# Two decoder layers, fp32 split products, one core: the rotary product leaves TensorE and the transfers exchange the halves

## The reference, cut to what matters

```python
def partial_rope(x, pos):
    half = ROPE_DIM // 2                     # 8
    ...
    x1, x2, rest = xf[..., :half], xf[..., half:ROPE_DIM], xf[..., ROPE_DIM:]
    out = jnp.concatenate([x1 * cos - x2 * sin, x2 * cos + x1 * sin, rest], axis=-1)
```

## Time and profile before

| | us |
|---|---|
| median of 3 runs | 1254.49 (1252.92 to 1254.75) |
| the profiled execution's own time | 1252.77 |
| its span, first to last instruction | 1251.0 |
| TensorE busy | 1235.3 |
| VectorE busy | 1028.7 |
| ScalarE busy | 699.1 |
| GpSimd busy | 172.2 |

### The profile page before, as it was taken

The page is one execution under the profiler, slowest core; times in us unless marked ns, Lnnn a source line. Parts: engine busy times, 40 slices in busy tenths (PEclk is TensorE's granted clock), DMA queues, the critical chain, the costliest instruction groups (busy, mean ns, idle before and its releaser), DMA issues.

```text
span 1251.0 us, 23751 instructions
## 1 busy us (share of the span) xinstructions
PE 1235.3 (99%) x9344; PEld 1182.2 (95%) x9344; DVE 1028.7 (82%) x1692; ACT 699.1 (56%) x1158; POOL 172.2 (14%) x120
## 2 busy tenths in 40 slices
PE   7999999999999999999999999999999999999999
PEld 7899999999999999999998989888899999998998
DVE  5787789578999999897655898885889999989865
ACT  6566547655555555763354774485655555558332
POOL 2464213100000000000015462131000000000000
DMA  5322210132332221223323222110322332222333
GB/s 196 98 74 69 68 35 21 49 118 85 115 122 102 102 102 69 69 102 118 110 94 100 92 68 69 34 52 18 134 102 102 118 119 102 102 69 85 118 118 118
DMA packets 27451, 113.74 MB, mean 91 GB/s; under 512 B 3664, under 2 KB 4304, under 8 KB 21968
## 3 DMA queue, kind: packets, MB, share of 16 engines
q1 hardware_dynamic: 26624, 111.18, 26.0%
q10 hardware_dynamic: 720, 1.09, 0.2%
HBM read 108.79 MB, written 2.10 MB: 89 GB/s over the span
## 4 chain that ended last, share of the span: by engine, by line
PE 90%; DVE 2%; POOL 2%; issue 1%; ACT 1%; DMA 0%; SPq 0%; POOLq 0%; DVEq 0%; ACTq 0%
PE ps L1390 22%; PE ps L1396 11%; PE ps L1005 10%; PE ps L1107 5%; PE ps L1101 5%; PE ps L1011 5%; PE ps L1102 5%; PE ps L1474 5%; PE ps L1510 4%; PE ps L1231 3%; PE ps L1479 2%; PE ps L1515 2%; PE ps L1204 1%; PE ps L1179 1%; PE ps L1214 1%
## 5 line engine op out<-in xcount | busy, mean ns | idle before, releaser
L1101 PE MATMUL ps<-xhi,whi 128*128 128x264 f32 (+1 forms) x616 | 174.3, 311 | 0.0
L1102 PE MATMUL ps<-xlo,whi 128*128 128x264 f32 (+1 forms) x616 | 167.5, 300 | 0.0
L885 POOL TENSOR_TENSOR wlo<-raw,whi 128x1024 fp32r<-128x1024 f32 x48 | 118.8, 2478 | 179.3 <-ACT whi L1688 178.7
L1101 PEld LDWEIGHTS ps<-xhi,whi 128*128 128x128 f32 x616 | 116.1, 188 | 4.8 <-issue 0.8
L1102 PEld LDWEIGHTS ps<-xlo,whi 128*128 128x128 f32 x616 | 116.2, 189 | 3.5
L1688 ACT ACTIVATE whi<-raw 128x1024 fp32r<-128x1024 f32 x74 | 77.9, 1054 | 48.3 <-PE ps L1011 29.9
L1107 PE MATMUL ps<-xhi,wlo 128*128 128x264 f32 (+1 forms) x616 | 100.6, 305 | 0.4 <-POOL wlo L885 0.4
L1107 PEld LDWEIGHTS ps<-xhi,wlo 128*128 128x128 f32 x616 | 85.3, 188 | 4.9 <-POOL wlo L885 0.6
L1390 PE MATMUL ps<-fhi,hi_a 128*128 128x264 f32 (+1 forms) x352 | 88.2, 283 | 0.0
L1390 PE MATMUL ps<-flo,hi_a 128*128 128x264 f32 (+1 forms) x352 | 88.1, 282 | 0.0
L1390 PE MATMUL ps<-flo,hi_b 128*128 128x264 f32 (+1 forms) x320 | 80.3, 283 | 0.0
(11 more groups left out here) (373 smaller groups left out, 3856.7 us busy)
## 6 DMA issues: line engine op xcount, KB each, us to landing
raw<-in_weights SPq DMA_DIRECT2D x116, 512.0 KB, 3.5
raw<-in_groups SPq DMA_DIRECT2D x42, 1024.0 KB, 4.8
out_hT<-h SPq DMA_DIRECT2D x7, 256.0 KB, 4.6
h<-in_hT SPq DMA_DIRECT2D x4, 264.0 KB, 6.2
h<-in_hT ACTq DMA_DIRECT2D x4, 264.0 KB, 5.9
cst<-in_consts SPq DMA_DIRECT2D x1, 780.5 KB, 9.3
xnb<-feat SPq DMA_DIRECT2D x20, 33.2 KB, 2.0
feat<-xnb SPq DMA_DIRECT2D x20, 33.2 KB, 2.0
```

Source lines behind the costliest of these rows:

```text
L885: nc.gpsimd.tensor_tensor(wlo[:, b], raw[:, b], whi[:, b].bitcast(F32), ALU.subtract).then_inc(split_done, 1)
L1101: nc.tensor.matmul(o, whi[:, k % 2, n], xhi[:, n, cut], start=(n == 0), stop=False)
L1102: nc.tensor.matmul(o, whi[:, k % 2, n], xlo[:, n, cut], start=False, stop=False)
```

## The change

The host lays the 16 rotated features of a head at every fourth row (0, 4, 8, ... of the 64), the two partners of a pair next to each other, and the gains of the norms likewise. `gather` copies a tile's 32 rotated rows in one transfer into buffer 0, and the same rows with partners exchanged in two transfers of 16 rows into buffer 1. TensorE's rotation step and its constant matrix are gone; VectorE multiplies buffer 0 by cosine, then waits for the exchanged rows and multiplies buffer 1 by a table of sines that carries the sign, and adds. `spread` puts 32 rows back in one transfer. The letters F leave TensorE's strings and the two digits of the rotation leave `BANKS_OF` in each layer; all other letters and digits are the same. The table of constants is 128 columns narrower.

```diff
-C_ID, C_ONE, C_BLK, C_ROT, C_COS, C_SIN = 0, 128, 256, 384, 512, 512 + N
+C_ID, C_ONE, C_BLK, C_COS, C_SIN = 0, 128, 256, 384, 384 + N
...
-ROPE_ROWS = (slice(48, 64), slice(112, 128))
+ROPE_ROWS = slice(0, 128, 4)
+ROPE_PAIR = (slice(0, 128, 8), slice(4, 128, 8))
...
-    "gather": (DMAE,), "rope": (PE, DVEE), "spread": (DMAE,), "split_k": (ACTE, DVEE),
+    "gather": (DMAE,), "rope": (DVEE,), "spread": (DMAE,), "split_k": (ACTE, DVEE),
...
-        self.packed = [sem(f"packed{n}_of{l}") for n in range(2)]
+        self.packed = sem(f"packed_of{l}")
+        self.exchanged = sem(f"exchanged_of{l}")
...
-                        sp.wait_ge(ev.spread[0], 16 * 6)
+                        sp.wait_ge(ev.spread[0], 16 * len(ROPED[0]))
+                    sp.dma_start(xnb[at:at + 32, 0], feat[ROPE_ROWS, place(k)]).then_inc(ev.packed, 16)
                     for hh in range(2):
-                        row = at + 16 * hh
-                        sp.dma_start(xnb[row:row + 16, 0], feat[ROPE_ROWS[hh], place(k)]).then_inc(ev.packed[n], 16)
+                        sp.dma_start(xnb[at + hh:at + 32:2, 1], feat[ROPE_PAIR[1 - hh], place(k)]).then_inc(ev.exchanged, 16)
 
                 def spread(n):
 
                     sp.wait_ge(ev.roped, n + 1)
                     for k in ROPED[n]:
-                        for hh in range(2):
-                            row = group_rows(k)[1] + 16 * hh
-                            sp.dma_start(feat[ROPE_ROWS[hh], place(k)], xnb[row:row + 16, 0]).then_inc(ev.spread[n], 16)
+                        row = group_rows(k)[1]
+                        sp.dma_start(feat[ROPE_ROWS, place(k)], xnb[row:row + 32, 0]).then_inc(ev.spread[n], 16)
...
-                def rope(n):
-                    b0, done = job_begin(("rope", n))
-                    pe.wait_ge(ev.packed[n], 32 * len(ROPED[n]))
-                    m = 32 * len(ROPED[n])
-                    for hf in range(2):
-                        ins = nc.tensor.matmul(bank(b0 + hf, HALF, slice(0, m)), cols(C_ROT, m, slice(0, m)),
-                                               xnb[0:m, 0, hf * HALF:(hf + 1) * HALF], start=True, stop=True)
                     ins.then_inc(done, 1)
 
...
-                    act.wait_ge(ev.spread[0], 16 * 6)
+                    act.wait_ge(ev.spread[0], 16 * len(ROPED[0]))
...
                 def rope(n):
-                    b0, taken, m = wait_done(("rope", n))
+                    tiles = sum(len(roped) for roped in ROPED[:n + 1])
                     dve.wait_ge(cst_loaded, 16 * (l + 1))
+                    dve.wait_ge(ev.packed, 16 * tiles)
                     rows = slice(0, 32 * len(ROPED[n]))
                     x, other = xnb[rows, 0], xnb[rows, 1]
-                    nc.vector.tensor_tensor(halves(other), two_banks(b0)[rows], halves(cols(C_SIN, N, rows)), ALU.mult).then_inc(taken, 1)
                     chain(nc.vector.tensor_tensor(x, x, cols(C_COS, N, rows), ALU.mult))
-                    dve.wait_ge(taken, m)
+                    dve.wait_ge(ev.exchanged, 32 * tiles)
+                    chain(nc.vector.tensor_tensor(other, other, cols(C_SIN, N, rows), ALU.mult))
                     nc.vector.tensor_tensor(x, x, other, ALU.add).then_inc(ev.roped, 1)
...
-def turned_last(w):
-
-    return np.roll(w.reshape(w.shape[0], -1, 64), -16, axis=2).reshape(w.shape)
+def turned_apart(w):
+
+    heads = w.reshape(w.shape[0], -1, 64)
+    out = np.empty_like(heads).reshape(w.shape[0], -1, 16, 4)
+    out[..., 0] = heads[..., :16].reshape(-1, heads.shape[1], 2, 8).swapaxes(2, 3).reshape(-1, heads.shape[1], 16)
+    out[..., 1:] = heads[..., 16:].reshape(w.shape[0], -1, 16, 3)
+    return out.reshape(w.shape)
...
-            p[l, :, c] = np.tile(np.roll(g[l], -16 if c in (P_DQ, P_DK) else 0), 2)
+            p[l, :, c] = np.tile(turned_apart(g[l][None])[0] if c in (P_DQ, P_DK) else g[l], 2)
...
-        c[r, C_COS:C_COS + N] = np.cos(ang[r % half])
-        c[r, C_SIN:C_SIN + N] = np.sin(ang[r % half])
-        c[r ^ half, C_ROT + r] = 1 if r // half % 2 else -1
+        c[r, C_COS:C_COS + N] = np.cos(ang[r // 2 % half])
+        c[r, C_SIN:C_SIN + N] = np.sin(ang[r // 2 % half]) if r % 2 else -np.sin(ang[r // 2 % half])
...
```

More of the change, by code:

```diff
@@ L223 @@
 PROJ_AT = [{s: n for n, s in enumerate(proj_halves(l))} for l in range(DEPTH)]
-AUX_KINDS = ("prenorm", "norm", "rope", "turn_tile", "gate", "index", "logits", "turn", "meta_turn", "turn_k", "gla_att", "gla_out",
+AUX_KINDS = ("prenorm", "norm", "turn_tile", "gate", "index", "logits", "turn", "meta_turn", "turn_k", "gla_att", "gla_out",
              "gla_kv", "back")
-WIDE_KINDS = ("prenorm", "norm", "rope", "turn_tile", "gate", "turn_k", "gla_att", "gla_out")
+WIDE_KINDS = ("prenorm", "norm", "turn_tile", "gate", "turn_k", "gla_att", "gla_out")
 def width_of(job):
@@ L257 @@
 STEPS_OF = (
[L258 to L261, removed]
+    {PE: "AAAAAAAAAAAABAAADAAAAAAAAAAAALAAAAAAAAADAMAAMDAAMMMMMMAAMAMAADAAAAAAADAPAAAAAAAAPAAXAXAAXADXAAALAaAL"
+     "AAbAdDAAAAAXAXAXXAXXAaAXAAYXYbMAXMAAAAAadMAMAZYZXYAXZYXZAYXbAAAAdZYXZAZYAAXLAPAZRAARPALYXAYAXMaAMabA"
+     "AAdLZZYAXYXZZbYAXYdZAAYAZZXXYXAYALXATSRSaAAATRTRSSATTaZbYXAdZADAZYAXYXDZYXAZbAYdDZAAAAYaZDYZAXXZAAXb"
+     "AYdAXAYXaZYXZYXZYXZbYadZYZYZfZbfdfff",
      ACTE: "ABCADAPALHIHACIADCIMIMDMMMMMMCAMMDAJCODIPIAJAPCXIIXDCXXALaPLADeJJXAXXXXAaXYYMMAXXXaMMYXeYYYAXPXeAYXK"
@@ L281 @@
 BANKS_OF = (
[L282 to L285, removed]
+    "0220230230123232020230130302030130130102310230020121021201320202020123020320301320130213031010130020"
+    "201202301201230320121203020230203013020301232",
+    "0222012032030032020123012301020201032013201302301320302020202020131020130113013031203103120103123012"
+    "320320120202301130130101302032013",
 )
@@ L1337, in out @@
                             low_pass(n, n, 2 * n + hf, parts[hf], mix_tiles, ks, True).then_inc(half_done, 2 // len(parts))
-                do = dict(prenorm=prenorm, proj=proj, norm=norm, rope=rope, turn_tile=turn_tile, turn_k=turn_k, gate=gate,
+                do = dict(prenorm=prenorm, proj=proj, norm=norm, turn_tile=turn_tile, turn_k=turn_k, gate=gate,
                           index=index, logits=logits, turn=turn, values=values, meta_turn=meta_turn,
@@ L1778, in split_q_hi @@
                     k, hh = SPLIT_Q[n]
-                    act.wait_ge(ev.spread[n // 4], 16 * (4 if n >= 4 else 6))
+                    act.wait_ge(ev.spread[n // 4], 16 * len(ROPED[n // 4]))
                     if n in SPLIT_AFTER:
@@ L1865, in fox_log @@
                     chain(nc.scalar.activation(fox_gate(), fox_gate(), ACT.Identity, bias=par[fox_rows, P_FB:P_FB + 1]))
-                    act.wait_ge(ev.spread[1], 16 * 4)
+                    act.wait_ge(ev.spread[1], 16 * len(ROPED[1]))
                     f = xnb[fox_rows, 0]
```

15 lines of the change are left out of this document (7 added, 8 removed).

## The result

The changed kernel takes 1256.54 us (median of 10 runs, 1255.64 to 1258.09) against 1254.28 us for the kernel before (10 runs beside it, 1252.91 to 1255.01): a ratio of 1.0019, 95% interval 1.0011 to 1.0027. It is slower by 2.3 us where 3.0 us less were forecast, and it lies above the range. The profiled execution took 1255.89 us, its span is 1254.0 us; the one before had 1252.77 and 1251.0 us.

What follows compares the result with a forecast made beforehand. The prediction took TensorE, busy 99% of the span, to bound the kernel. Gains of 0.5 + 1.2 (layer 0) and 0.2 + 1.1 (layer 1) make 3.0 us: 1254.49 to 1251.5 us, range 1248.4 to 1254.3 us.

Steps and rivals of the forecast that it cites:

- What the change offers: TensorE time around the four rotation products: 1.85 and 1.71 us in layer 0, 1.27 and 1.24 in layer 1, 6.07 in all.
- SyncE's queue: Gather and spread transfers: strided rows issue in 0.62 us and land in 2.0 us; the later unit load costs nothing.
- Layer 0, 1.7 us forecast: Both rotations of layer 0: 1.7 us gained, between 0.5 and 3.56 us.
- the chain from the projection halves: Layer 0, ScalarE to VectorE up to the first index scores: only 0.5 us of 1.85 us is left.
- the forecast wait of 0.5 us: Layer 0, norm of unit 6: TensorE, 2.2 us ahead, meets GpSimd's squares with 1.7 us of slack; waits about 0.5 us.
- so 0.2 us of 1.27 us is left: Layer 1, first rotation: GpSimd's subtraction holds one VectorE operation, the turn of SMALL waits about 1 us; gain 0.2 us.
- The lock: Layer 1, first rotation: VectorE operations with two SBUF inputs contend with GpSimd's subtraction; without it, 1.1 us better.
- Layer 1, second rotation, 1.1 of 1.24 us forecast: VectorE's unbroken run moves only 0.2 us, returning rows come over 1 us earlier; gain 1.1 us, not under 0.2.
- D: Rival: SyncE takes longer to issue strided rows, up to 1.10 us each; 4.7 us slower, 1259.2 us; chance 0.08.
- C: Rival: the lock does not bite in layer 1; gain 4.1 us, 1250.4 us; chance 0.15.
- A: Rival: all offered time arrives, 6.07 us, giving 1248.4 us; chance 0.13.
- B: Rival: mostly given back, in layer 0 the sum meets GpSimd's squares; gain 1.4 us, 1253.1 us; chance 0.27.

Runs made afterwards that it cites:

- e1: Kernel before with the new row layout and one packing and one return transfer per tile, product kept in both layers: 1250.20 us, ratio 0.9968.
- e12: Same kernel as e1, run again beside e9 to e11: 1250.62 us, ratio 0.9971.
- e8: Changed kernel with the change in layer 0 alone; layer 1 keeps its product, with the new layout: 1252.34 us, ratio 0.9986.
- e10: e8 with GpSimd's subtraction for unit 7 in layer 0 held until VectorE has split the keys: 1250.19 us, ratio 0.9968.
- e3: Changed kernel with GpSimd's subtraction for unit 5 in layer 1 put after the first rotation's sum: 1252.65 us, ratio 0.9992.
- e2: Changed kernel with VectorE's two copies of unit 3 put ahead of layer 1's first rotation: 1254.49 us, ratio 1.0004.
- e5: Kernel before with VectorE's sine product of layer 1's first rotation done seven times instead of once: 1260.36 us, ratio 1.0052.
- e4: Changed kernel with GpSimd's subtractions for units 4 and 5 in layer 1 put after the first rotation: 1254.09 us, ratio 1.0003.
- e9: Layer 0 as in e1 (new layout, product kept), layer 1 as in e7 (no product): 1249.83 us, ratio 0.9964.
- e11: e7 with GpSimd's subtraction for unit 7 in layer 0 held until VectorE has split the keys: 1250.25 us, ratio 0.9967.
- e7: e4 with SyncE's spread of the first group in layer 1 put ahead of the unit load: 1251.96 us, ratio 0.9983.

## Why the prediction was wrong

**What the change offers.** The product is gone, with its 16 records; and TensorE's rows bear out the time offered: it gets ahead by 1.8 us at each product of layer 0 and by 1.28 us at the first of layer 1 (1.85, 1.71 and 1.27 us offered).

**SyncE's queue** was costed rightly for layer 0: issue 0.59 us, landing 2.0 us, and the load behind the gathers, issued 2 us later, delays nothing that a trace shows. At the first gathers of layer 1 the landing is longer, 2.7 us in the median and up to 4.5 us (before 2.7 and 3.6). That the cosine product still began at 664.08 us, inside the forecast 663.9 to 664.4, is luck: the last tile's packed rows were issued at 660.70 us and not near 661.8, since layer 0 had ended earlier, and took 3.4 us instead of 2.0. What the step missed is the worth of packing with one transfer, a part of this change: 1.5 us in layer 0. With the order of VectorE and GpSimd that came with it, e1 and e12 are 3.8 and 3.6 us under before with the product in place. Of the 1.85 us offered at the first product, 0.73 were a wait for transfers that half as many issues remove.

**Layer 0, 1.7 us forecast.** Measured 1.75 in the table, 1.6 by e8; the sum knows no lower clock, which takes 1.0 us off it in some executions. The size was right and its reasons only half. I put the loss at the first index scores down to the chain from the projection halves, where only 0.5 us could be had. TensorE did wait there, 1.1 us; but e10 shows that 2 us of the chain are a subtraction in its way, in the kernel before too, where the split that I took for the chain's own length stood at 2.91 us for work of 0.70. I had read the 0.23 us of waiting behind it and not the row itself. At the norm of unit 6 the forecast wait of 0.5 us came, as 0.8 us, but for ScalarE's relu of an index score and not for GpSimd's squares.

**Layer 1, first rotation, "so 0.2 us of 1.27 us is left": this step failed.** The lock was foreseen, with its place and size (cosine product forecast until 667.1, it ended at 665.76, 1.35 us earlier with the whole layer; turn's wait about 1.1 us; e3, which has that one hold alone, waits 1.4 us). But I let one subtraction meet the rotation, the one that stood there before, and kept the next at its old 668.75. It waits for ScalarE's rounding, that waits for TensorE's buffer, and TensorE was what the change made earlier, against the layer's own beginning by 1.28 us, the very time I was counting as gain. So it came at 666.12 and held the sum as well, and the turn waited 3.3 us. To this came 1.6 us of lower clock, of which the prediction has nothing. In the profiled executions of e2, after, and e5 the clock fell here behind waits of 2.15, 3.3 and 3.8 us, and in those of e3 and e4 with 1.42 and 1.80 us it didn't. The length of a wait does not settle it, though: in layer 0 it fell behind 1.1 us in three executions out of seven. e3 takes out the second hold and with it both costs: 3.9 us by the medians, 3.6 us with each against the kernel before beside it, of the 5.0 us between the forecast and the result.

The Trainium skill (page "SBUF — State Buffer", section "Who interferes with whom") had the rule, that two SBUF inputs on VectorE contend with a GpSimd instruction that reads SBUF; the traces agree, 1.68 and 2.75 us instead of 0.71. It was applied to the instructions as they stood and not as the change would move them.

**Layer 1, second rotation, 1.1 of 1.24 us forecast.** It gave nothing. VectorE's run is unbroken there, and it came late from the first rotation, by 2.2 us (its second rotation starts at 697.45 instead of 695.23); TensorE waits 0.9 us for it. Even in e9 and e11, where the first rotation is in order, that wait of 0.9 us stands. So the term was too large by most of itself, and not only by what came from in front. The rows point to the same step as in the first rotation: the prediction let VectorE's run move as one piece, and it grew. In after, e3, e7, e9 and e11 GpSimd's subtraction and squares hold two of its operations (2.05 and 1.13 us, shown above) that take 0.48 and 0.23 us where layer 1 keeps its product, and the stretch takes 9.95 to 9.97 us. With the new layout and the product (e1, e8, e10, e12) it is 9.2 to 9.4 us, and TensorE, later by the product, does not wait. That the growth is what makes the wait is read from the traces; no run moved that subtraction or those squares.

**The rivals.** D is out by the issues' durations; C by the lock's biting; A by e11, where with no subtraction in the way of layer 1's first rotation and the key splits the whole change is still only level with the layout alone. B had the right sign of the correction, but it let squares meet a rotation in layer 0; they did (1.88 us for the sum at 63.48), yet TensorE's next wait, at the norm, was for ScalarE's relu and not behind that sum. None of the rivals let the change's own gain move a held operation; the range ended 2.2 us below the result.

**What stays open.** Layer 1 with the new layout and its product takes 0.1 to 1.0 us longer than before (71.06 to 72.00 against 70.98 us). TensorE waits 0.4 (e12), 0.9, 1.0 and 1.2 us (e1) for the packing there, and 0.2 us before. But e5, with the old layout, has 1.0 us too, and e1 and e12 are one kernel, so this may be scatter of the landing and not the layout. Whether the transfer lands late beside the weight loads was not tried. Nor do these runs tell why the clock fell in layer 0 in some executions and not in others.

## What to carry to other kernels

When work is taken off the engine that bounds, shift every later event that waits for it, on all engines, before asking which of them meet: the buffers come free sooner, and so do the subtractions that hold VectorE. Where a GpSimd instruction with a fixed place must not meet a chain on VectorE, a wait on the end of that chain costs little (some 3.6 and 2.2 us came back here); if a load waits for that instruction, what queues behind the load on SyncE has to be moved too (e4 and e7). Look at what each part of a change is worth alone: here the layout made the gain (1250.2 us) and the part it was made for, no product, adds to it nothing that these runs can tell.

## What the runs showed of the hardware

One VectorE operation can be held several times its length when subtractions follow each other closely: 5.24 us for a pair of splits that takes 1.44 us unheld and 3.17 us with one subtraction in the way. And an idle TensorE can pay twice: after 3.3 us of waiting the granted clock was 0.50 for some 3 us, at a cost of 1.6 us; after 3.8 us (with 1.0 us shortly before) it was 0.50 for 6 us. After waits of 1.1 and 0.7 us it fell in three executions, for some 3 us and 1.0 us of time, and stayed at 1.00 in four.
